# One-hot tiles of a product-key gate: written token by token, contiguously, instead of four tokens interleaved

## The reference, cut to what matters

```python
experts = (jnp.take_along_axis(i1, ci // PEER_TOPK, axis=-1) * PEER_N_KEYS
           + jnp.take_along_axis(i2, ci % PEER_TOPK, axis=-1))
gate = jax.nn.softmax(top_s, axis=-1).astype(xn.dtype)
...
act = jax.nn.gelu(jnp.einsum('thkd,td->thk', u, xb), approximate=False)
return jnp.einsum('thk,thkd->td', gb * act, v_tab[eb])
```

## Time and profile before

| what | value |
|---|---|
| median of 3 runs | 3289.77 us (3286.05 to 3306.37) |
| the profiled execution, its span | 3288.7 us |
| PE busy | 2939.5 us, 89% of the span |
| DVE busy | 2132.3 us, 65% |
| POOL busy | 1847.5 us, 56% |
| ACT busy | 1109.3 us, 34% |

### The profile page before, as it was taken

How to read it: one execution, slowest core, us unless ns; L and a number is a source line. 1 busy time by engine, 2 the same in 40 slices (tenths; PEclk the granted TensorE clock), 3 DMA queues, 4 the chain that set the end, 5 groups by cost and what they waited for, 6 DMA issues and landing times. The chain is left out here.

```text
span 3288.7 us, 46850 instructions
## 1 busy us (share of the span) xinstructions
PE 2939.5 (89%) x15784; PEld 1644.6 (50%) x15880; DVE 2132.3 (65%) x3995; ACT 1109.3 (34%) x1480; POOL 1847.5 (56%) x1490
## 2 busy tenths in 40 slices
PE   6955878989999999989999999599999887999887
PEld 3422574445555555567777776344444333444333
DVE  2595486311377688767777774467777766777777
ACT  4311335222344444445555553311122211122122
POOL 1396354011244533455555556588778885877785
PEclk9987877999999999999999999899999998999999
DMA  3200001211133333357777777799999996998996
GB/s 115 70 0 32 7 0 52 84 51 38 55 113 112 112 112 112 112 204 254 270 255 261 263 251 270 252 326 327 329 322 334 343 339 232 337 319 314 330 320 261
DMA packets 260395, 648.59 MB, mean 197 GB/s; under 512 B 16992, under 2 KB 115552, under 8 KB 257136
## 3 DMA queue, kind: packets, MB, share of 16 engines
q1 hardware_dynamic: 186176, 378.33, 32.5%
q0 software_dynamic: 74160, 269.52, 22.8%
HBM read 542.39 MB, written 105.91 MB: 197 GB/s over the span
## 5 line engine op out<-in xcount | busy, mean ns | idle before, releaser
L91 POOL TENSOR_TENSOR w_low<-w_ring,w_high 128x1024 f16<-128x1024 f32 x164 | 484.1, 2953 | 989.9 <-ACT w_ring L86 989.9
L1230 PE MATMUL psum<-region_y,w_high 128*128 128x384 f16 x2048 | 672.4, 328 | 18.2 <-POOL w_low L91 16.6
L1649 PE MATMUL psum<-vh,wh 128*128 128x512 bf16 x1504 | 584.1, 388 | 106.0 <-POOL wl L1698 73.3
L1232 PE MATMUL psum<-region_y,w_low 128*128 128x384 f16 x2048 | 670.7, 327 | 0.0
L1231 PE MATMUL psum<-region_y,w_high 128*128 128x384 f16 x2048 | 670.4, 327 | 0.0
L1650 PE MATMUL psum<-vl,wh 128*128 128x512 bf16 x1504 | 583.8, 388 | 38.1 <-POOL wl L1698 36.1
L1651 PE MATMUL psum<-vh,wl 128*128 128x512 bf16 x1504 | 583.2, 388 | 1.7
L1665 ACT ACTIVATE vh<-w_ring 128x1024 bf16<-128x1024 f32 x128 | 135.0, 1055 | 894.6 <-DMA w_ring<-in_v_t_dram 868.3
L1760 DVE TENSOR_TENSOR region_x<-region_x,psum 128x1024 f32<-128x1024 f32 x192 | 234.0, 1219 | 145.8 <-PE psum L1651 145.5
L1649 PEld LDWEIGHTS psum<-vh,wh 128*128 128x128 bf16 x1536 | 153.2, 100 | 340.4 <-issue 139.1
L1694 POOL TENSOR_TENSOR vl<-w_ring,vh 128x1024 bf16<-128x1024 f32 x128 | 272.9, 2133 | 41.7 <-ACT vh L1665 40.9
(11 more groups left out here) (234 smaller groups left out, 5022.5 us busy)
## 6 DMA issues: line engine op xcount, KB each, us to landing
w_ring<-in_u_t_dram SPq DMA_DIRECT2D x128, 512.0 KB, 3.8
w_ring<-in_v_t_dram SPq DMA_DIRECT2D x128, 512.0 KB, 7.0
acts_dram<-ge SPq DMA_DIRECT2D x128, 384.0 KB, 2.8
gates_dram<-scores SPq DMA_DIRECT2D x24, 2048.0 KB, 7.3
gt<-gates_dram SPq DMA_DIRECT2D x32, 1536.0 KB, 9.5
at<-acts_dram SPq DMA_DIRECT2D x32, 1536.0 KB, 13.1
w_ring<-in_w_stream_dram SPq DMA_DIRECT2D x20, 512.0 KB, 3.2
w_ring<-in_w_q_dram SPq DMA_DIRECT2D x16, 512.0 KB, 3.2
```

The source lines that it names most:

```text
L91: pool.tensor_tensor(self.wl[:, s, :], self.wf[:, s, :], self.wh[:, s, :], ALU.subtract).then_inc(self.w_lo, 1)
L1230: pe.matmul(a, uh[:, par, row], xh[:, n, cols], start=(n == 0), stop=False)
L1232: last = pe.matmul(a, ul[:, par, row], xh[:, n, cols], start=False, stop=(n == KC - 1))
L1649: pe.matmul(a, wh[:, par, c, rows], vh[:, par, c, cols], start=(c == 0), stop=False)
```

## The change

The one-hot tiles of a token become contiguous: `hot` now has the order `r n t i`, with three tiles per token (the one-hot of i1, and the second one-hot already times the gate's high and low part); the unweighted one-hot of i2 is not written any more. Each tile is written by one `tensor_scalar` instruction over 128 elements for one token: a compare of the contiguous index row `iota_1` with the token's index, for the gated tiles followed in the same instruction by the product with the gate part. Index and gate come as scalars that are read per partition from memory ([P, 1] operands, float32). For that, `tokens_of` copies, once per turn, the indices and gate parts of the turn's 64 tokens to the float32 tile `of_token`, and waits for the copies. The wait `two_hot` is gone. PE reads contiguous operands; the number, size and order of its instructions are unchanged.

```diff
-    hot = flat[:, 2 * NK * GT:2 * NK * GT + 2 * 4 * P * OCT // 2].bitcast(BF16).rearrange(
-        "p (r n q i t) -> p r n q i t", r=2, n=4, q=2, i=P)
+    hot = flat[:, 2 * NK * GT:2 * NK * GT + 2 * 3 * P * OCT // 2].bitcast(BF16).rearrange(
+        "p (r n t i) -> p r n t i", r=2, n=3, t=OCT)
...
-    iota_4 = flat[:, at:at + P * QUAD // 2].bitcast(BF16).rearrange("p (q i t) -> p q i t", q=1, t=QUAD)
+    iota_1 = flat[:, at:at + P // 2].bitcast(BF16)
+    at += P // 2
+    TURN = LOOP * 2 * OCT
+    of_token = flat[:, at:at + 4 * TURN].rearrange("p (n t) -> p n t", n=4)
...
-                        for part in (2, 3):
-                            last = pe.matmul(psum[:, 4 + 2 * r + b, t * P:(t + 1) * P], hot[:, r, 0, b, :, t],
-                                             hot[:, r, part, b, :, t], start=(part == 2), stop=(part == 3))
+                        for part in (1, 2):
+                            last = pe.matmul(psum[:, 4 + 2 * r + b, t * P:(t + 1) * P], hot[:, r, 0, QUAD * b + t, :],
+                                             hot[:, r, part, QUAD * b + t, :], start=(part == 1), stop=(part == 2))
...
+            def tokens_of(n):
+
+                tokens = ds(TURN * n + GATHERED * P, TURN)
+                dve.tensor_copy(of_token[:, 0:2, :], picks[:, :, tokens])
+                dve.tensor_copy(of_token[:, 2:4, :], parts[:, :, tokens]).then_inc(turn_ok, 1)
+                dve.wait_ge(turn_ok, n + 1)
+
             def octet(n, o):
 
                 r = o % 2
-
-                def per_token(ap):
-                    return ap.rearrange("p (q a t) -> p q a t", q=2, a=1).to_broadcast([P, 2, P, QUAD])
-
-                iota = iota_4.to_broadcast([P, 2, P, QUAD])
-
-                tokens = ds(8 * OCT * n + (OCT * o + GATHERED * P), OCT)
-
                 after(dve, g_mm, 8 * n + (o - 1))
-                dve.tensor_tensor(hot[:, r, 1], iota, per_token(picks[:, 1, tokens]), ALU.is_equal).then_inc(two_hot, 1)
-                dve.tensor_tensor(hot[:, r, 0], iota, per_token(picks[:, 0, tokens]), ALU.is_equal)
-                dve.wait_ge(two_hot, 8 * n + (o + 1))
-                dve.tensor_tensor(hot[:, r, 2], hot[:, r, 1], per_token(parts[:, 0, tokens]), ALU.mult)
-                dve.tensor_tensor(hot[:, r, 3], hot[:, r, 1], per_token(parts[:, 1, tokens]),
-                                  ALU.mult).then_inc(hot_ok, 1)
+                for t in range(OCT):
+                    i = OCT * o + t
+                    dve.tensor_scalar(hot[:, r, 0, t, :], iota_1, of_token[:, 0, i:i + 1], None, ALU.is_equal)
+                    for part in (1, 2):
+                        last = dve.tensor_scalar(hot[:, r, part, t, :], iota_1, of_token[:, 1, i:i + 1],
+                                                 of_token[:, 1 + part, i:i + 1], ALU.is_equal, ALU.mult)
+                last.then_inc(hot_ok, 1)
...
-            dve.tensor_copy(iota_4.rearrange("p q i t -> p (q i) t"), iota_x[:, :, 0:QUAD])
+            dve.tensor_copy(iota_1, iota_x[:, :, 0])
...
             def turn(n):
+                tokens_of(n)
                 for j in range(LOOP):
                     octet(n, 2 * j)
                     octet(n, 2 * j + 1)
                     take(LOOP * n + j, j % 2, (LOOP // 2) * n + j // 2)
```

More of the change, by code:

```diff
@@ L1142, in select_and_activate @@
     tile = flat[:, 0:2 * NK * GT].rearrange("p (u c t) -> p u c t", u=2, c=NK)
-    hot = flat[:, 2 * NK * GT:2 * NK * GT + 2 * 4 * P * OCT // 2].bitcast(BF16).rearrange(
-        "p (r n q i t) -> p r n q i t", r=2, n=4, q=2, i=P)
-    at = 2 * NK * GT + 4 * P * OCT
+    hot = flat[:, 2 * NK * GT:2 * NK * GT + 2 * 3 * P * OCT // 2].bitcast(BF16).rearrange(
+        "p (r n t i) -> p r n t i", r=2, n=3, t=OCT)
+    at = 2 * NK * GT + 3 * P * OCT
     iota_x = flat[:, at:at + P * OCT // 2].bitcast(BF16).rearrange("p (i t) -> p i t", t=OCT)
     at += P * OCT // 2
-    iota_4 = flat[:, at:at + P * QUAD // 2].bitcast(BF16).rearrange("p (q i t) -> p q i t", q=1, t=QUAD)
+    iota_1 = flat[:, at:at + P // 2].bitcast(BF16)
+    at += P // 2
+    TURN = LOOP * 2 * OCT
+    of_token = flat[:, at:at + 4 * TURN].rearrange("p (n t) -> p n t", n=4)
     ge_st = [sems(f"ge_st{s}") for s in range(2)]
@@ L1154, in select_and_activate @@
     chosen, found = sems("tk_chosen"), sems("tk_found")
-    iota_in, pre, two_hot, hot_ok, g_mm, g_ok = (sems(n) for n in (
-        "iota_in", "g_pre", "two_hot", "hot_ok", "g_mm", "g_ok"))
+    iota_in, pre, turn_ok, hot_ok, g_mm, g_ok = (sems(n) for n in (
+        "iota_in", "g_pre", "turn_ok", "hot_ok", "g_mm", "g_ok"))
     STEPS = 23
```

## The result

The change made the kernel slower: 3424.98 us (4 runs, 3424.26 to 3428.6) against 3291.84 us before, a ratio of 1.041 (95% interval 1.038 to 1.043). The forecast was 3442 us, in a range of 3375 to 3560. The profiled execution's span is 3426.4 us, 137.7 us more than that of before.

The account below looks back on a forecast made before the run. PE bounds slots 64 to 111; DVE was to replace it: 9.6 + 2.65 + 0.2 + 2.1 = 14.6 us a slot, 0.1 for waits, so 706 us instead of 554, 152 more. Forecast 3442 us, range 3375 to 3560.

Parts of the forecast that it names:

- The bound moves to VectorE: In slots 64 to 111 VectorE needs 14.6 us a slot against TensorE's 10.3 and becomes the bound; chance 0.70.
- Price of a tile: On VectorE an ungated tile costs 161 ns and a gated one 220, together 9.6 us a slot where there were 4.8.
- errata rule: VectorE instruction: 58 cycles plus elements by pace, 94 ns a tile; VectorE's slot 9.5 us, PE staying the bound.
- `tokens_of`: Its two added copies per turn on VectorE were put at 0.7 us, 0.2 us a slot.
- POOL's hold: POOL's forming of the weights' low part (L91) keeps VectorE waiting 2.1 us a slot, bounds 1.0 and 2.3.
- TensorE hidden in full: In slots 64 to 111 TensorE's gain is hidden in full, and it waits some 4 us a slot.
- The gain within reach: Contiguous operands save PE at most 0.062 us for each of 1536 octet matmuls, 95 us, while PE stays the bound.
- Rival 1: Scalar reads on VectorE hide behind each other, a tile costs 105 ns, PE stays the bound: 3230 us; chance 0.10.
- the wait for rows: VectorE's 46.2 us of waiting for fetched rows in slots 64 to 111 goes, with 3 us more a slot to land.
- Its variant: PE's octet matmuls stay at 0.117 us because the stride was not their cause: 3290 us; chance 0.02.
- Rival 2: VectorE's compare with scalar runs below four elements a step: at two 3513 us, chance 0.12; at one 3668 us, 0.03.
- Rival 3: PE's pauses lower its clock and PE becomes the bound at the lower one: 3725 us; chance 0.03.

Follow-up runs that it names:

- e6: The kernel after with a constant in place of the gate part, so every tile reads one scalar from memory; 3334.2, 3335.2 us, stage 595.1 us.
- e7: The kernel after with POOL forming only half of each weight column's low part in slots 64 to 111; 3377.6 us, stage 641.6 us.
- e5: The kernel after with constants in place of the token's index and gate in all tiles; stage 520.3 us, ratio to before 0.990.
- e8: The kernel before with two tokens interleaved instead of four and row fetches issued one slot earlier; 3194.9 us, ratio 0.973, stage 460.4 us.
- e1: The kernel before with both of PE's operands read as contiguous tiles; 3249.2 us, ratio 0.988, stage 522.1 us.
- e3: The kernel before with only the weights read contiguously by PE; 3282.2 us, ratio 0.999, stage 549.2 us.
- e4: The kernel before with two tokens interleaved instead of four, still four long VectorE instructions per octet; 3250.9 us, ratio 0.989, stage 515.4 us.
- e9: The kernel before with only the row fetches issued one slot earlier; 3287.2 us, ratio 1.001, stage 552.3 us.
- e2: The kernel before with only the moving operand read contiguously by PE; 3250.3 us, ratio 0.988, stage 522.5 us.

## Why the prediction was right

**The bound moves to VectorE.** Right: 98% busy, and e6 and e7 each shortened the stage by just what they took off VectorE.

**Price of a tile.** Expected 161 and 220 ns; the timeline gives 0.16 and 0.225 us. With constants a tile costs 0.10 us (35 + 70 = 105 expected); how these divide into elements and fixed part, no run separates. One scalar adds 0.06 us (e6's duration 248 against e5's 190 ns), the second as much again (305). By the errata rule of the Trainium skill (VectorE: DVE Perf Modes, "The TRN2 errata") the estimate was 94 ns with or without such scalars. The runs agree within a tenth for constants and show more than twice as much for two scalars. That gap alone turned a gain into a loss: e5's stage is 520 us, the kernel after's 687, before's 552.

**`take`, `tokens_of`, POOL.** `take` and the step to the next octet stayed near 2.65 us (2.62 us, from 1708.25 to 1710.87). `tokens_of` was put at 0.7 us a turn and takes some 0.9 (in e6, 0.39 us of idle time and 0.50 from its first copy to the first tile), 2 us more in the stage. POOL's hold was put at 2.1 us and is 1.87; that is the largest error of the sum, 48 x 0.23 = 11 us. The 0.1 us a slot allowed for VectorE's waits, 5 us, wasn't needed either. Against these, the tiles cost 9.76 us a slot and not 9.6, 8 us more in the stage. A slot thus costs some 14.5 us instead of 14.7. The stage is 687 us where 706 were expected, in part also because VectorE writes the first octet's tiles ahead of it. That 3425 lies only 17 us below 3442 owes something to luck, since these errors have both signs.

**TensorE hidden in full.** Right, but sized wrongly: the octet's matmuls were put at 0.078 us apart, the middle of 0.055 and 0.099, and stand 0.056 apart. A weight load of 99 ns is no bound on the spacing; it overlaps. Hidden as it was, this didn't touch the sum. TensorE's longest wait was 7.3 us where 3 to 5 were expected, and its busy share 0.79 where 0.7 was, because it ran partly at the lower clock. The gain within reach, put at 95 us at most, shows in e8: 552.2 - 460.4 = 92 us.

**The rivals.** Rival 1 (scalars free) would have needed a mean of 0.135 us per tile; it was 0.20. Its price of 3230 us was not the time such a kernel would have had either: e5 shows a stage of 520 us, 32 less than before, because the wait for rows would have taken over, and 458 without that wait. Its variant falls by e1 to e3. The rule on strides that was cited for it (the Trainium skill, SBUF — State Buffer, "Door 1: The DMA port swizzle") does not agree with the measurement, which decides: a stride of four bfloat16 elements is not free for the moving operand (0.117 us a matmul instead of 0.056), one of two nearly is. Rival 2, as it was priced, falls by e5: at two elements a step a tile with constants would start 0.136 us behind the last, and they start 0.10 us apart. Rival 3's mechanism is there, a clock of 0.66 over the 5 us behind a pause. It makes TensorE's matmuls of the stage last 541 us instead of e8's 454, some 1.8 us a slot where 2.6 were reckoned, and costs nothing there, as reckoned.

**What was overlooked** is the wait for rows as the next bound. In the forecast it was only said to vanish, which it did, since VectorE became slower. Had VectorE not become the bound, it would have been the next one, as e1, e4 and e5 show.

## What to carry to other kernels

When an instruction is split into short ones, price each from start to start: a fixed part and the elements (together 0.10 us for 128 here), and each scalar read from memory (about 60 ns here), and set the sum against the idle time of that engine, not against its busy share. If a layout hurts TensorE, look for the smallest change that stops it hurting: two neighbours together were enough for both engines here. And a gain on the engine that bounds a stage is worth as much as the distance to the next wait; look up the hidden waits first, since removing one may be worth nothing alone (e9) and 1.6% of the kernel's time once the engine that hid it is faster (e8 against e4).

## What the runs showed of the hardware that was not expected

- The moving operand's stride decides nearly alone: 294 to 297 ns at a stride of four elements, 218 at two and 219 at one. The weights' stride made no difference to the stage with a contiguous moving operand (522.1 and 522.5 us) and 3 us of 552 with a strided one.
- 128 x 128 matmuls with a weight load of 98 ns each run 0.056 us apart (e1).
- In `tensor_scalar` a second operation costs nothing (248 ns with and without in e6, 190 in e5); a second scalar from memory costs as much as the first (248 to 305 ns, after 190 to 248).
- GpSimd can be kept waiting for very long by a dense run of two-input instructions on VectorE. In the mixer, VectorE runs 120 products of 1024 elements one behind the other (L550). In e5 a low part of the weights began 0.36 us behind the first of them and ended 2 us behind the last; VectorE's row, GpSimd's (that low part and the next), all of e5's low parts (min/median/max ns), and TensorE's wait:

```profile
129.30 143.59 DVE L550 SCALAR_TENSOR_TENSOR region_y<-glu,par,region_y 128x1024 f32<-128x1024 f32 x120
```

```profile
129.66 147.29 POOL L91 TENSOR_TENSOR w_low<-w_ring,w_high 128x1024 f16<-128x1024 f32 x2 [3.17 <-ACT w_ring L86]
```

```profile
L91 POOL TENSOR_TENSOR w_low<-w_ring,w_high x164: 2114/2131/145212, 34.3 to 2125.3; 128x1024 f16<-128x1024 f32 x164
```

```profile
PE psum L399 <- POOL w_low L91: 139.0, 2, 137.8
```

  145 us instead of 2.1. The longest such wait is 121 us in the profile of before, 67 in that of after. TensorE's wait for it (L399) is 139 us in e5 and e7, 74 to 75 in before and e2, 61 in the other eight profiles; the first octet starts at 1489 to 1492 us, at 1423 to 1424, and at 1409 to 1414. The differences match, 78 and 14 us; that the one causes the other was not tried. A dense run is not enough by itself: in the kernel after five low parts got in between the same products within 2.3 to 3.1 us before one was held for 67, and among the tiles of the octets POOL got in at once (2127 ns on average). What makes the difference stays open.
